# A fused three-layer transformer kernel: reordered splits in the last two differential heads, a reordered delta-rule prologue, and both gate projections ahead of the last transposition

## The chip, the cores and the metric

The program runs on one core of one Trainium2 chip. The metric is the device time of one execution in microseconds (us); smaller is better. Several executions of one program are timed, and their median stands for it.

## The reference

One batch of 256 tokens with 1024 channels goes through two layers of a first block (latent attention, then differential attention, each followed by a feed-forward network with a three-tap convolution) and one hybrid layer (causal attention and a gated delta rule side by side, joined by gates). Everything is float32. Cut to what the change touches:

```python
def diff_mixer(x, w_qkv, lam_p, subln_g, w_o, layer_idx):   # 8 heads, 2 x 64
    sc = jnp.einsum('bqhjd,bkhjd->bhjqk', qb, k) * scale - slopes * dist
    p = jax.nn.softmax(sc, -1)
    a = p[:, :, 0] - lam * p[:, :, 1]
    o = rms_norm(jnp.einsum('bhqk,bkhd->bqhd', a, v), subln_g) * (1.0 - lam_init)
    return o.reshape(b, s, H * 2 * d) @ w_o

def gated_deltanet(q, k, v, g, beta):                       # 8 heads, chunks of 64
    q, k = l2norm(q) * dk ** -0.5, l2norm(k)
    decay = exp(G[i] - G[j]) for j <= i                     # G: running sum of g
    m = strict_lower((k * beta) @ k.T * decay)
    u, w = solve(I + m, [v * beta, k * beta * exp(G)])
    qk = lower(q @ k.T * decay)
    # then chunk after chunk: v_new = u - w @ S; o = q_dec @ S + qk @ v_new; S = ...

def hybrid_layer(x, ...):
    proj = rmsnorm(x) @ w_in         # q, k, v, z of attention and of the delta rule, gates
    y_a = (attention(q_a, k_a, v_a) * silu(z_a)) @ w_branch_a
    y_b = (rmsnorm(gated_deltanet(silu(conv(...)), g, beta)) * silu(z_b)) @ w_branch_b
    merged = sigmoid(gate_a) * y_a + sigmoid(gate_b) * y_b
    return x + rmsnorm(merged @ w_out)
```

## The kernel before, in words

**Precision and weights.** Each float32 product is made of three TensorE matmuls on a "high" part (the value rounded to a shorter format) and a "low" part (the rest): high by high, high by low, low by high. Every weight matrix comes from memory in chunks of 128 x 1024 into one of six slots (`raw0` to `raw5`). ScalarE writes `high` (line 357), then VectorE or GpSimd writes `low = raw - high` (line 368); this pair is called the split of a chunk. A table of phases (`Phase(...)`) says which slots a stage uses, how many chunks each has, and whose low parts GpSimd makes (`gpsimd_low`; for the differential stage slots 1 and 3, for the following feed-forward stage `ffn1` only slot 3, for the delta rule all). `refill(split, p, k, i)` splits the chunk that follows chunk i of slot k, which is the first of the next stage behind the last.

**What orders the work.** Every engine has a program written out by hand, and runs it in order. Semaphores tell it when a producer is done (`wait_ge`). The SyncE queue (SP) issues the weight loads in order too: a load waits for the low part of the chunk before it in its slot (`low_done`), and all later loads wait behind it.

**Places that the change touches.**

- `diff_pe`, `diff_act`, `diff_dve`, `diff_pool` hold the eight differential heads. Heads 0 to 5 run in `head`, heads a = 6 and b = 7 in `last_heads`. For a head: `scores` (line 1240), VectorE's `take_scores` and `maxima`, ScalarE's `exponentials` (1328), VectorE's `weights` (1425 to 1431, whose end is semaphore `p`), `turn_prob` on TensorE (1248), `take_prob` on ScalarE (1334), `result` (1256), then mean square (1399), root on GpSimd (1488), norm (1404), `turn_result` (1227), `result_high` (1323) and `result_low` (1410), and `add_output` into `acc`. Behind head b stands `rows_out_end` (440 to 448) and the boundary: residual, norm and transposition for the next stage.
- `gdn_pe`, `gdn_act`, `gdn_dve`, `gdn_pool` hold the delta rule. A prologue makes the gates and the inputs of the first pair of heads; then `pair_*` runs four times. In the prologue the convolved q and k are transposed (`turn_pe`, 1754), ScalarE squares them, VectorE sums (`squares_dve`, 1827 and 1828), GpSimd takes the root (`root_pool`, 1902), VectorE scales (`norm_dve`, 1849, semaphore `tk`), TensorE transposes back (`back_pe`, 1769), ScalarE copies (`back_act`, 1808), TensorE multiplies keys and queries (`products_pe`, 1782), VectorE masks (`masked_keys_dve`, 1866), TensorE transposes the mask product (`turn_m_pe`, 1790), ScalarE copies it (`mt_act`, 1813) and VectorE makes the first inverse (`init_rows_dve`, `init_dve`, 1885 to 1898). The mask comes from `decay_dve` (1839 to 1843), `decay_act` (1802) and `mask_pool` (1909 to 1914). `pair_pe` begins with `level_x` (1937), which waits for the last step of `init_dve`. Projections `gdn_block(x, e, j, part)` (1686; x: 0 q, 1 k, 2 v, 3 z; e: head of the pair j; part: half of 24 matmuls) fill the time between. `spin` (505) are matmuls whose result is not used.
- `load_pairs` orders the loads of this stage in the SP queue; slots 0, 1, 2 are q, k, v, slots 3 and 4 the z weights of even and odd heads.
- `att_pe`'s last head (7) of the causal attention: `out_project(pe, 0, ...)`, `att_turn_prob` (2469), `out_project(pe, 1, ...)`, `att_result` (2475). ScalarE's `att_take_prob` stands between the last two.

## Time and profile before

| what | value |
| --- | --- |
| median of 3 executions (lowest, highest) | 1084.79 us (1082.2, 1086.27) |
| the profiled execution's own time | 1084.68 us |
| its span, first to last instruction | 1082.9 us |
| mean granted TensorE clock | 0.991 of full speed |
| TensorE matmul busy | 1046.0 us (97%) |
| VectorE, ScalarE, GpSimd busy | 668.1, 561.0, 417.5 us (62, 52, 39%) |
| DMA | 162.27 MB, mean 150 GB/s |
| chain that ended last, by engine | PE 79%, POOL 6%, issue 6%, DVE 5%, ACT 3%, DMA 2% |

The span is the stretch from the first to the last instruction; 1.8 us of the execution lie around it. PE is TensorE, DVE VectorE, ACT ScalarE, POOL GpSimd. TensorE is busy nearly throughout, so what is left to look for are the few stretches in which it idles or runs at a lower granted clock. An overlapped matmul's duration is longer than its distance to the next one.

### The profile page before, as it was taken

What the parts mean: (1) busy time and instruction counts of PE and PEld (TensorE: products, weight loads), DVE (VectorE), ACT (ScalarE), POOL (GpSimd) and SP (SyncE); (2) the same over time, 40 slices, a digit from 0 to 9 for tenths busy, and PEclk for the clock granted to TensorE, in tenths of its full rate; (3) what the DMA queues carried; (4) which work ended last, traced back from release to release, by engine and by line L of the source; (5) the groups of instructions that cost most, each with busy time, mean ns of one, the idle gap of its engine ahead of it and who ended that gap; (6) DMA issues with size and microseconds to landing.
All of it is one profiled execution on the core that took longest, in us unless ns stands there. A gap on an engine that the chain in (4) does not pass through costs nothing.

```text
span 1082.9 us, 21787 instructions
## 1 busy us (share of the span) xinstructions
PE 1046.0 (97%) x8224; PEld 957.7 (88%) x8224; DVE 668.1 (62%) x1073; ACT 561.0 (52%) x1022; POOL 417.5 (39%) x284
## 2 busy tenths in 40 slices
PE   9899999999999999899999999899999999999997
PEld 7799689999978998599999978799999899999996
DVE  4555766766675556777666755566676555544444
ACT  5455565555564666555555556434533355544443
POOL 1000234334342333333343364656654365534331
PEclk9999999999999999999999999899999999999999
DMA  8334466565544443366655542233323235436551
GB/s 326 118 108 134 147 200 193 177 210 185 178 139 141 149 143 110 103 228 177 205 184 170 173 148 90 98 101 116 99 60 115 82 130 156 152 112 218 191 181 48
DMA packets 46136, 162.27 MB, mean 150 GB/s; under 512 B 5248, under 2 KB 5504, under 8 KB 45952
## 3 DMA queue, kind: packets, MB, share of 16 engines
q1 hardware_dynamic: 44784, 156.78, 44.2%
q0 software_dynamic: 1296, 4.72, 1.5%
q8 instruction: 38, 0.62, 0.2%
q14 instruction: 18, 0.15, 0.0%
HBM read 160.43 MB, written 1.05 MB: 149 GB/s over the span
## 4 chain that ended last, share of the span: by engine, by line
PE 79%; POOL 6%; issue 6%; DVE 5%; ACT 3%; DMA 2%; SPq 0%; DVEq 0%; POOLq 0%; ACTq 0%
PE work L399 12%; PE work L401 12%; PE work L400 12%; PE work L1686 8%; PE acc L399 5%; PE acc L400 5%; PE acc L401 5%; PE work L2407 4%; POOL low L368 4%; PE work L2419 2%; PE acc L2419 2%; PE acc L1951 1%; PE acc L1937 1%; ACT high L357 1%; PE acc L1953 1%
## 5 line engine op out<-in xcount | busy, mean ns | idle before, releaser
L368 POOL TENSOR_TENSOR low<-raw,high 128x1024 fp32r<-128x1024 f32 x109 | 264.8, 2432 | 303.5 <-ACT high L357 303.5
L368 DVE TENSOR_TENSOR low<-raw,high 128x1024 fp32r<-128x1024 f32 (+3 forms) x183 | 272.7, 1498 | 163.3 <-ACT high L357 163.2
L357 ACT ACTIVATE high<-raw 128x1024 fp32r<-128x1024 f32 (+2 forms) x293 | 299.8, 1032 | 47.3 <-DMA raw<-in_w_out 26.1
L399 PE MATMUL work<-xh,high 128*128 128x256 f32 (+1 forms) x1032 | 291.6, 283 | 0.7 <-DVE low L368 0.7
L400 PE MATMUL work<-xl,high 128*128 128x256 f32 (+1 forms) x1032 | 288.8, 280 | 0.0
L401 PE MATMUL work<-xh,low 128*128 128x256 f32 (+1 forms) x1032 | 288.7, 280 | 0.0
L399 PEld LDWEIGHTS work<-xh,high 128*128 128x128 f32 (+1 forms) x1032 | 194.2, 188 | 7.7 <-issue 4.8
L400 PEld LDWEIGHTS work<-xl,high 128*128 128x128 f32 (+1 forms) x1032 | 194.3, 188 | 2.3 <-issue 0.6
L401 PEld LDWEIGHTS work<-xh,low 128*128 128x128 f32 (+1 forms) x1032 | 194.1, 188 | 0.2
L1157 POOL TENSOR_TENSOR h<-gelu,cv 128x256 f32<-128x256 f32 x44 | 49.2, 1118 | 202.1 <-ACT gelu L1077 108.3
L1686 PE MATMUL work<-xh,high 128*128 128x256 f32 x256 | 77.4, 302 | 2.2 <-DVE hn L1741 2.2
L1686 PE MATMUL work<-xl,high 128*128 128x256 f32 x256 | 72.5, 283 | 0.0
L1686 PE MATMUL work<-xh,low 128*128 128x256 f32 x256 | 72.3, 282 | 0.0
L399 PE MATMUL acc<-high,hh 128*128 128x512 f32 x168 | 66.0, 393 | 2.0 <-DVE low L368 1.2
L400 PE MATMUL acc<-low,hh 128*128 128x512 f32 x168 | 65.9, 392 | 0.0
L401 PE MATMUL acc<-high,hl 128*128 128x512 f32 x168 | 65.4, 390 | 0.0
L1083 ACT ACTIVATE hh<-h 128x256 fp32r<-128x256 f32 x44 | 18.4, 418 | 70.2 <-POOL h L1157 70.2
L1686 PEld LDWEIGHTS work<-xh,high 128*128 128x128 f32 x256 | 48.8, 191 | 4.9 <-issue 2.4
L1071 ACT ACTIVATE cv<-work,vec 128x256 f32<-128x256 f32 x44 | 24.8, 564 | 51.0 <-PE work L401 51.0
L1686 PEld LDWEIGHTS work<-xh,low 128*128 128x128 f32 x256 | 49.0, 191 | 0.0
L1686 PEld LDWEIGHTS work<-xl,high 128*128 128x128 f32 x256 | 48.9, 191 | 0.0
L1159 POOL TENSOR_TENSOR hl<-h,hh 128x256 fp32r<-128x256 f32 x44 | 34.4, 782 | 24.4 <-ACT hh L1083 24.4
(386 smaller groups left out, 2220.9 us busy)
## 6 DMA issues: line engine op xcount, KB each, us to landing
raw<-in_w_ffn SPq DMA_DIRECT2D x132, 512.0 KB, 4.3
raw<-in_w_out SPq DMA_DIRECT2D x39, 512.0 KB, 4.4
raw<-in_w_att SPq DMA_DIRECT2D x32, 512.0 KB, 3.7
raw<-in_w_diff SPq DMA_DIRECT2D x31, 512.0 KB, 4.2
raw<-in_w_gdn SPq DMA_DIRECT2D x24, 512.0 KB, 3.7
raw<-in_w_mla SPq DMA_DIRECT2D x8, 512.0 KB, 3.5
raw<-in_w_gdnz SPq DMA_DIRECT2D x8, 512.0 KB, 3.6
raw<-in_w_mla SPq DMA_DIRECT2D x8, 384.0 KB, 3.1
```

Of the source, the lines that this page charges most:

```text
L357: act.activation(high[k][:, 0:w], raw[k][:, 0:w], ACT.Copy).then_inc(high_done[k], 1)
L368: eng.tensor_tensor(low[k][:, 0:w], raw[k][:, 0:w], high[k][:, 0:w], ALU.subtract).then_inc(low_done[k], 1)
L399: pe.matmul(out, lhs[0], rhs[0], start=start, stop=False)
L400: pe.matmul(out, lhs[0], rhs[1], start=False, stop=False)
L401: return pe.matmul(out, lhs[1], rhs[0], start=False, stop=stop)
L1071: act.activation((cg, cv)[value][j][:], W[bank][:, 0:TOK], ACT.Identity, scale=ffn_taps(layer, i, j, value, 1, 0), bias=ffn_taps(layer, i, ...
L1083: act.activation(hh[j][:], h32[j][:], ACT.Copy).then_inc(f[j]["hh"], 1)
L1157: pool.tensor_tensor(h32[j][:], gelu[j][:], cv[j][:], ALU.mult).then_inc(s["h32"], 1)
L1159: pool.tensor_tensor(hl[j][:], h32[j][:], hh[j][:], ALU.subtract).then_inc(s["hl"], 1)
L1686: last = pe.matmul(W[x][:, 0:TOK], l[slot][:, b * P:(b + 1) * P], r[:, b, :], start=(s == 0), stop=(s == 23))
L2407: last = pe.matmul(W[0][:, t * TOK:(t + 1) * TOK], x[:, b, t * P:(t + 1) * P], w[k][:, o:o + TOK], start=(b == 0 and term == 0), stop=(b = ...
L2419: last = pe.matmul(out, w[k][:, b * P:(b + 1) * P], x[:, b, :], start=(s == 0), stop=(s == 23))
```

## The change

It edits four places. (1) In the last two differential heads ScalarE takes the transposed probabilities before it splits the first feed-forward chunk of slot 0, and its other splits move one place later; GpSimd no longer makes the low part for the first `ffn1` chunk of slot 1 (VectorE does, behind `result_low(b)`), and it waits for head b's `weights` before the low part of slot 3. (2) In the delta rule's prologue the orders of TensorE, ScalarE, VectorE and GpSimd change, four spin matmuls go, and the copy of the gate rows is cut in two functions. (3) The load of slot 2's third chunk is issued one place earlier. (4) In the last attention head both gate projections stand ahead of the transposition of the probabilities.

```diff
@@ -1359,21 +1359,21 @@
             exponentials(a)
             take_qk(b, W[1])
             result_high(a - 1, W[0][:, TOK:2 * TOK])
+            take_prob(a, W[1])
             refill(split, ph["diff"], 0, b)
-            take_prob(a, W[1])
-            refill(split, ph["diff"], 1, b)
             squares(a)
             exponentials(b)
             refill(split, ph["diff"], 3, a - 1)
-            split(ph["ffn1"], 4, 0)
+            refill(split, ph["diff"], 1, b)
             take_values(b)
             take_prob(b, W[2])
             result_high(a)
             squares(b)
             refill(split, ph["diff"], 2, b)
-            split(ph["ffn1"], 5, 0)
+            split(ph["ffn1"], 4, 0)
             result_high(b)
             refill(split, ph["diff"], 3, a)
+            split(ph["ffn1"], 5, 0)
 
         act.wait_ge(d["lam"], 1)
         refill(split, ph["diff"], 0, 0)
@@ -1471,6 +1471,7 @@
             result_norm(b)
             refill(split, ph["diff"], 2, b)
             result_low(b)
+            refill(split, ph["diff"], 1, b)
 
         dve.wait_ge(d["lam"], 5)
         for k in (0, 1):
@@ -1497,9 +1498,8 @@
                 refill(split, ph["diff"], 3, i - 1)
 
         def last_heads(a, b):
-            pool.wait_ge(high_done[1], ph["ffn1"].base[1] + 1)
-            pool.tensor_tensor(low[1][:], raw[1][:], high[1][:], ALU.subtract).then_inc(low_done[1], 1)
             result_root(a)
+            pool.wait_ge(h["p"], b + 1 + DIFF_SEEN)
             refill(split, ph["diff"], 3, a - 1)
             result_root(b)
 
@@ -1578,7 +1578,10 @@
 
     def gates_rows_act(act):
         act.wait_ge(z_["pe"], 3)
+        act.wait_ge(e_["cums"], 1)
         act.activation(cum_all[:], acc[:].rearrange("p a (c k) -> p (a c) k", c=4), ACT.Copy).then_inc(z_["act"], 1)
+
+    def gates_grown_act(act):
         act.activation(grown_all[:], acc[:].rearrange("p a (h t k) -> p (a h) t k", h=2, t=NT)[:, :, 1, :],
                        ACT.Exp).then_inc(z_["act"], 1)
 
@@ -1840,6 +1843,8 @@
         if not is0(j):
             dve.wait_ge(e_["be"], j)
         dve.tensor_scalar(dec_l[:], dcum, 0.0, None, ALU.max)
+        if is0(j):
+            squares_dve(dve, 0)
         dve.tensor_scalar(dec_u[:], dcum, 0.0, None, ALU.min).then_inc(e_["dd"], 1)
 
     def norm_dve(dve, j):
@@ -1878,8 +1883,6 @@
         masked_dve(dve, 1).then_inc(e_["mk"], 1)
 
     def init_rows_dve(dve, j):
-        if is0(j):
-            dve.memset(inv_t[HALF:P, :, 0:HALF], 0.0)
         dve.wait_ge(e_["mk"], 2 * j + 1)
         for h_ in HALVES:
             last = dve.tensor_tensor(bm[h_, 0, :, 0:HALF].rearrange("p (e t) k -> p e t k", e=2), mk[h_, :, 0, :, h_],
@@ -2074,13 +2077,11 @@
         turn_pe(pe, 0)
         block_pe(pe, 3, 0)
         block_pe(pe, 2, 1)
+        back_pe(pe, 0)
         gdn_block(pe, 3, 1, 0, 0)
-        back_pe(pe, 0)
+        products_pe(pe, 0)
+        turn_m_pe(pe, 0)
         gdn_block(pe, 3, 1, 0, 1)
-        products_pe(pe, 0)
-        spin(pe, A[1], 2)
-        turn_m_pe(pe, 0)
-        spin(pe, A[1], 2)
         for i in range(PAIRS):
             pair_pe(pe, i)
 
@@ -2169,15 +2170,16 @@
         block_high_act(act, split, 1, 1, 0)
         for e in range(2):
             squares_act(act, 0, e)
-        decay_act(act, 0)
         gates_rows_act(act)
         z_tanh_act(act, 0, 0)
-        block_high_act(act, split, 3, 0, 0)
+        decay_act(act, 0)
+        gates_grown_act(act)
         block_mid_act(act, 2, 1, 0)
         back_act(act, 0)
+        block_high_act(act, split, 3, 0, 0)
+        mt_act(act, 0)
         z_tanh_act(act, 1, 0)
         block_high_act(act, split, 2, 1, 0)
-        mt_act(act, 0)
         block_high_act(act, split, 3, 1, 0)
         for i in range(PAIRS):
             pair_act(act, i)
@@ -2298,15 +2300,15 @@
         block_taps_dve(dve, 1, 1, 0)
         block_silu_dve(dve, 1, 1, 0)
         decay_dve(dve, 0)
-        gates_key_dve(dve)
-        squares_dve(dve, 0)
         z_silu_dve(dve, 0, 0)
         norm_dve(dve, 0)
-        z_silu_dve(dve, 1, 0)
+        gates_key_dve(dve)
+        dve.memset(inv_t[HALF:P, :, 0:HALF], 0.0)
         masked_keys_dve(dve, 0)
         init_rows_dve(dve, 0)
         init_dve(dve, 0)
         masked_queries_dve(dve, 0)
+        z_silu_dve(dve, 1, 0)
         for i in range(PAIRS):
             pair_dve(dve, i)
 
@@ -2364,10 +2366,10 @@
         block_low_pool(split, 1, 1, 0)
         root_pool(pool, 0)
         mask_pool(pool, 0)
+        pool.wait_ge(e_["init_g"], 1)
+        grow_pool(pool, 0)
         block_low_pool(split, 3, 0, 0)
         block_low_pool(split, 2, 1, 0)
-        pool.wait_ge(e_["init_g"], 1)
-        grow_pool(pool, 0)
         block_low_pool(split, 3, 1, 0)
         for i in range(PAIRS):
             pair_pool(pool, i)
@@ -2501,10 +2503,9 @@
                     att_queries_keys(pe, i + 1, part)
             else:
                 out_project(pe, 0, 0, xh, xl)
-            att_turn_prob(pe, i)
-            if not more:
                 pe.wait_ge(h["vev"], HEADS + ATT_SEEN)
                 out_project(pe, 1, 0, xh, xl)
+            att_turn_prob(pe, i)
             if more:
                 for part in range(2):
                     att_values(pe, i + 1, part)
@@ -2878,11 +2879,14 @@
                     for k in (0, 1):
                         if c > 2:
                             load(sp, p, k, c)
+                if j == 0:
+                    load(sp, p, 2, 2)
                 if j + 2 < PAIRS:
                     load(sp, pz, 3, j + 2)
                 else:
                     load_first(ph["att"], 3)
-                load(sp, p, 2, 2 * j + 2)
+                if j > 0:
+                    load(sp, p, 2, 2 * j + 2)
                 if j + 2 < PAIRS:
                     load(sp, pz, 4, j + 2)
                 load(sp, p, 2, 2 * j + 3)
```

What the order of instructions becomes is shown at three places. First GpSimd in the last two differential heads, behind the loop (`COMPARE_AND_BRANCH`); line 1488 (1489 after) is the root of a head, 368 a low part. Before:

```order
L466 COMPARE_AND_BRANCH
L1501 TENSOR_TENSOR low<-raw,high 128x1024
L1488 TENSOR_TENSOR stat<-mean,vec 128x2
L368 TENSOR_TENSOR low<-raw,high 128x1024
L1488 TENSOR_TENSOR stat<-mean,vec 128x2
L601 TENSOR_TENSOR stat<-mean,vec 128x1 x2
```

and with the change:

```order
L466 COMPARE_AND_BRANCH
L1489 TENSOR_TENSOR stat<-mean,vec 128x2
L368 TENSOR_TENSOR low<-raw,high 128x1024
L1489 TENSOR_TENSOR stat<-mean,vec 128x2
L601 TENSOR_TENSOR stat<-mean,vec 128x1 x2
```

The first low part is gone from GpSimd, and the root of head a comes first. Second, VectorE in the prologue, from the decay differences to the masked keys. Before:

```order
L1839 TENSOR_TENSOR bm<-acc,gate_cum 128x512
L1842 TENSOR_SCALAR dec_l<-bm 128x512
L1843 TENSOR_SCALAR dec_u<-bm 128x512
L1611 TENSOR_TENSOR gate_bg<-gate_eg,gate_beta 128x16
L1827 TENSOR_REDUCE ssq<-sq 128x8
L1828 TENSOR_SCALAR mean<-ssq 128x8
L1741 SCALAR_TENSOR_TENSOR hn<-tanh_z,work 128x256
L1849 TENSOR_TENSOR qk_tok<-work,root 128x512 x2
L1741 SCALAR_TENSOR_TENSOR hn<-tanh_z,work 128x256
L1866 TENSOR_TENSOR mk<-acc,mask_e 128x2x256
```

and with the change:

```order
L1842 TENSOR_TENSOR bm<-acc,gate_cum 128x512
L1845 TENSOR_SCALAR dec_l<-bm 128x512
L1830 TENSOR_REDUCE ssq<-sq 128x8
L1831 TENSOR_SCALAR mean<-ssq 128x8
L1848 TENSOR_SCALAR dec_u<-bm 128x512
L1744 SCALAR_TENSOR_TENSOR hn<-tanh_z,work 128x256
L1854 TENSOR_TENSOR qk_tok<-work,root 128x512 x2
L1614 TENSOR_TENSOR gate_bg<-gate_eg,gate_beta 128x16
L2306 MEMSET inv_t 64x4x64
L1871 TENSOR_TENSOR mk<-acc,mask_e 128x2x256
```

The sum of squares and its mean now stand between the two decay parts, and the second gate silu (`hn`) leaves the stretch. Third, ScalarE in the same prologue, from the squares to the copy of the transposed mask product. Before:

```order
L1796 ACTIVATE sq<-work 128x512 x2
L1802 ACTIVATE dec_l<-dec_l 128x512
L1803 ACTIVATE dec_u<-dec_u 128x512
L1581 ACTIVATE cum_all<-acc 128x2048
L1582 ACTIVATE grown_all<-acc 128x1024
L1711 ACTIVATE tanh_z<-work 128x256
L357 ACTIVATE high<-raw 128x1024
L1696 ACTIVATE conv<-work,vec 128x256
L1808 ACTIVATE silu<-work 128x2x256
L1809 ACTIVATE silu<-work 128x2x256
L1711 ACTIVATE tanh_z<-work 128x256
L357 ACTIVATE high<-raw 128x1024
```

and with the change:

```order
L1799 ACTIVATE sq<-work 128x512 x2
L1582 ACTIVATE cum_all<-acc 128x2048
L1714 ACTIVATE tanh_z<-work 128x256
L1805 ACTIVATE dec_l<-dec_l 128x512
L1806 ACTIVATE dec_u<-dec_u 128x512
L1585 ACTIVATE grown_all<-acc 128x1024
L1699 ACTIVATE conv<-work,vec 128x256
L1811 ACTIVATE silu<-work 128x2x256
L1812 ACTIVATE silu<-work 128x2x256
L357 ACTIVATE high<-raw 128x1024
L1816 ACTIVATE mt<-work 128x512
L1714 ACTIVATE tanh_z<-work 128x256
```

The large copy `cum_all` moves ahead of the exponentials, and a split that stood ahead of the copy-back (`silu`, lines 1808 and 1811) now stands behind it.

## Rows read from the trace of the kernel before

**Rows 1.** Waits of TensorE, whole run: who waited <- whom: us, times, longest
```profile
PE work L515 <- DVE hn L547: 4.6, 6, 1.9
...
PE acc L1937 <- DVE inv L1898: 1.7, 1, 1.7
```

**Rows 2.** Windows: stretch, length, busy of PE, PEld, DVE, ACT, POOL; granted clock, DMA share, GB/s
```profile
425.00:430.00 5.00, 3.08 (x23) 2.36 (x22) 4.41 (x9) 3.30 (x6) 0.00 (x0) 1.00 0.80 314
438.03:441.57 3.54, 3.36 (x16) 2.99 (x17) 1.37 (x4) 1.07 (x2) 0.00 (x0) 0.55 0.41 143
700.00:704.00 4.00, 3.98 (x46) 3.71 (x48) 2.37 (x5) 0.39 (x1) 3.47 (x3) 0.65 0.02 4
964.00:968.00 4.00, 4.00 (x23) 4.00 (x22) 0.82 (x1) 0.49 (x1) 0.00 (x0) 0.57 0.79 262
700.01:744.12 44.11, 44.10 (x520) 41.55 (x520) 27.94 (x59) 17.59 (x32) 25.58 (x17) 0.96 0.31 97
744.12:787.16 43.04, 43.04 (x527) 40.53 (x526) 30.63 (x63) 19.66 (x35) 27.49 (x18) 1.00 0.32 99
```

**Rows 3.** Timeline of PE, last heads: start, duration, [idle before <- releaser]
```profile
428.85 0.35 PE L1256 MATMUL work<-v_sb,prob_t 128*128 128x128 f32 x1 [1.30 <-issue]
...
438.03 0.44 PE L1248 MATMUL work<-const,prob 128*128 128x128 f32 x2 [2.48 <-DVE prob L1431]
```

**Rows 4.** Lines L1399 and L1428 on DVE: ns min/median/max over all heads
```profile
L1399 DVE TENSOR_SCALAR mean<-stat x8: 169/171/1957, 347.2 to 442.6; 128x2 f32<-128x2 f32 x8
...
L1428 DVE TENSOR_SCALAR prob<-prob,soft x16: 347/353/2453, 340.7 to 434.6; 128x256 f32<-128x256 f32 x16
```

**Rows 5.** Timeline of POOL, last heads
```profile
430.40 2.40 POOL L1501 TENSOR_TENSOR low<-raw,high 128x1024 fp32r<-128x1024 f32 x1 [8.32 <-ACT high L357]
...
434.47 2.44 POOL L368 TENSOR_TENSOR low<-raw,high 128x1024 fp32r<-128x1024 f32 x1
```

**Rows 6.** Timeline of ACT, last heads and the first row of the boundary behind them
```profile
427.21 1.06 ACT L357 ACTIVATE high<-raw 128x1024 fp32r<-128x1024 f32 x1 [1.17 <-DMA raw<-in_w_ffn]
...
428.18 0.58 ACT L1334 ACTIVATE prob_t<-work 128x512 f32<-128x512 f32 x1
...
432.20 0.50 ACT L1328 ACTIVATE prob<-prob,soft 128x256 f32<-128x256 f32 x1
...
447.24 0.60 ACT L574 ACTIVATE xh<-acc 128x512 fp32r<-128x512 f32 x1 [0.86 <-PE acc L448]
```

**Rows 7.** Timelines of the prologue: PE, DVE, POOL, DVE, ACT, ACT
```profile
687.07 0.36 PE L1686 MATMUL work<-xh,high 128*128 128x256 f32 x1 [2.22 <-DVE hn L1741]
...
679.70 2.62 DVE L1843 TENSOR_SCALAR dec_u<-bm 128x512 f32<-128x512 f32 x1
...
683.83 1.68 POOL L1902 TENSOR_TENSOR root<-mean,vec 128x8 f32<-128x8 f32 x1 [1.78 <-DVE mean L1828]
...
686.84 1.28 DVE L1849 TENSOR_TENSOR qk_tok<-work,root 128x512 f32<-128x512 f32 x2
...
691.22 0.60 ACT L1808 ACTIVATE silu<-work 128x512 f32<-128x512 f32 x1 [3.44 <-PE work L1769]
...
696.96 1.06 ACT L357 ACTIVATE high<-raw 128x1024 fp32r<-128x1024 f32 x1 [3.95 <-DMA raw<-in_w_gdn]
```

**Rows 8.** The same steps in the second pair: chain of waits (products), then timeline of DVE
```profile
737.84 1.79 PE acc L1782 x16
...
739.66 0.69 DVE L1866 TENSOR_TENSOR mk<-acc,mask_e 128x512 f32<-128x512 f32 x1 [1.84 <-PE acc L1782]
...
743.03 0.42 DVE L1898 TENSOR_TENSOR inv<-const,work 128x256 f32<-128x256 f32 x1
```

**Rows 9.** DVE instructions with two operands in SBUF: L1858 by line, one L368 by timeline
```profile
L1858 DVE TENSOR_TENSOR kdec<-qk_tok,gate_kd x4: 416/416/418, 705.9 to 834.6; 128x256 f32<-128x256 f32 x4
...
940.32 2.20 DVE L368 TENSOR_TENSOR low<-raw,high 128x1024 fp32r<-128x1024 f32 x1 [1.39 <-ACT high L357]
```

**Rows 10.** Timeline of PE, last attention head
```profile
963.74 0.67 PE L2469 MATMUL work<-const,causal_prob 128*128 128x128 f32 x3 [2.04 <-DVE causal_prob L2641]
```

## The prediction

> **What bounds the kernel.** I read the shares of busy time first: TensorE is busy for 97% of the span, so only its idle stretches and its clock can give time back. The list of its waits comes next. Its largest entry belongs to the boundaries between stages (4.6 us in six waits), which the change does not edit; of the others, the one ahead of the first pair of the delta rule is 1.7 us long [rows 1]. Its timeline shows the rest: 1.30 us and 2.48 us in the last two differential heads [rows 3], 2.22 us in the prologue [rows 7], 2.04 us in the last attention head [rows 10]. Then I read windows for the granted clock. After three of them (2.48, 1.73, 2.04 us) the clock falls from 1.00 to a mean of 0.55 to 0.65, that is to its lower level of 1.2 GHz, for about 4 us; after 1.30 us it stays at 1.00 [rows 2]. So each long idle costs twice: the first pair of heads takes 44.11 us, the next one 43.04 us [rows 2].
>
> **Part 1, the last two differential heads.** TensorE's transposition of head b's probabilities waits 2.48 us, to 438.03 [rows 3]. What makes them late is VectorE: a mean that takes 0.17 us in most heads once took 1.96 us, and a scaling of 0.35 us once took 2.45 us [rows 4]. Both lie against a GpSimd low part: 430.40 to 432.80 and 434.47 to 436.91 [rows 5]. The change takes the first off GpSimd and puts the second behind these weights. VectorE then has 1.8 + 2.1 = 3.9 us less to do. Part of the 1.8 is hidden by ScalarE's exponentials, which end at 432.7 [rows 6]; behind them stand about 2 us of short VectorE work, so the weights are ready near 434.7. TensorE itself is free at 438.03 - 2.48 = 435.55 [rows 3], or, since ScalarE's copy of head a's probabilities no longer stands behind a split (it started at 428.18, after one that began at 427.21 [rows 6], while the transposition ended at 427.55), 0.55 us earlier: 435.0. The wait vanishes. First term: 2.5 + 0.55 = 3.0 us.
>
> The low clock behind it goes as well. The stretch 438.03 to 441.57 ran at 0.55 [rows 2]; it is a chain of short transpositions, copies and one product. At full clock I take 2.4 us for its 3.54: half as long would be 1.8, unchanged 3.5. Second term: 1.1 us (bounds 0 and 1.7).
>
> Price: ScalarE now has two splits behind `result_high(b)`, before one. It was idle 0.86 us there [rows 6], a split takes 1.06 us, and the load for the first of them is issued when GpSimd's low part ends (436.91, which is not earlier than before). I take 0.3 us (bounds 0 and 1). VectorE's added low part stands in the same idle time ahead of `acc`: nothing, and if that cover is gone, at most its 1.2 us. Slot 1's next load waits for it but stands behind slot 2's in the queue: nothing. Part 1: 3.0 + 1.1 - 0.3 = 3.8 us.
>
> **Part 2, the prologue.** Before, the squares' mean stood behind the second decay part, which waited on GpSimd's third low part and ended at 679.70 + 2.62 = 682.32; the root began at 683.83 [rows 7]. Now the sum (some 1.2 us) stands ahead of it, so the mean is out when that low part ends, at 682.2 to 682.6. From there the chain is: root 1.7 (to 684.3), norm 1.28 (685.5) [rows 7], transposition back 0.9 (686.4), ScalarE's two copies 2 x 0.6 [rows 7] less their overlap (687.5), products 1.8 [rows 8] (689.4), and from the masking to the first inverse what the second pair shows, 739.66 to 743.45 = 3.8 [rows 8]. The first `level_x` starts at 693.2 at the latest and 692.9 at the earliest, against 700.01. ScalarE's copy of the gate rows now runs while VectorE sums, and the mask, GpSimd's next work behind the root, has the 5 us until the products end. TensorE has 4.8 us of projections and products in there and idles three times, 0.7, 0.9 and 0.8 us: shorter than the 1.30 after which the clock stayed. The spins (3.8 us of busy time) are no work and cost nothing to leave out. First term: 7.0 us. Second: the first pair at full clock, 44.11 - 43.04 = 1.1 us [rows 2].
>
> Price: GpSimd now does three low parts (7.1 us) without a pause from 692.4, where `kdec` and `kbg` follow at 697.1, just as the third begins. The row of `kdec` shows 0.416 to 0.418 us in all pairs, never beside a low part; a VectorE low part that met one took 2.20 us [rows 9], one alone 1.2. By the first row the price is 0, by the second up to 2.3 us on VectorE, of which TensorE's half projection hides about 1.1. I take 1.1, because `kdec` reads two SBUF tiles as the low part does. The Trainium skill ("SBUF — State Buffer", section "SBUF: two separate sides") says that a VectorE instruction with two SBUF inputs and a GpSimd instruction that reads SBUF lock each other out for a whole instruction. By that rule the price stands; by the `kdec` row alone the sum would be 1.1 us larger.
>
> The load of slot 2's third chunk no longer waits behind slot 3's, for which ScalarE waited 3.95 us, to 696.96 [rows 7], before it could copy the transposed mask product. Its gain is inside the 7.0. Slot 3's load is issued 3 us later, at 694.7, some 20 us before its split. Nothing. Part 2: 7.0 + 1.1 - 1.1 = 7.0 us.
>
> **Part 3, the last attention head.** The second gate projection covers the 2.04 us wait that ended at 963.74 [rows 10]: TensorE reaches the transposition at 964.2. What is late next is ScalarE's copy behind it, an idle of 0.6 us. The 24 matmuls of the second projection took 4.6 us at a mean clock of 0.57 [rows 2], against 3.15 for the first. Sum: 2.04 + 1.45 - 0.6 + 0.3 (the slow transposition) = 3.2 us; bounds 2 and 3.5.
>
> **Sum.** 3.8 + 7.0 + 3.2 = 14.0 us. From the profiled execution's 1084.68 us (0.1 below the median) that gives 1070.7 us. The scatter of the three executions, 4 us, is wider than 0.1, and a change under 0.5% (5.4 us) cannot be told from none.
>
> **Rivals.** (A) The clock falls all the same. The new prologue has three idles within 8 us and the spins are gone. For it: 1.73 us behind spins was enough at 700 [rows 1, 2]. Against: 1.30 us did not do it. Price: the 1.1 us of the first pair, and about 1.4 us in the prologue: 1073.2 us. The skill ("TensorE: Matmul & The Clock Gate", "What's actually happening") holds that the low level is the default and activity lifts it; that speaks for A, and against taking spins out. (B) Part 1 is given back at the boundary: ScalarE's split, VectorE's low part and a new fall of the clock among short idles take 3 us. 1073.7 us. (C) Only one place works, because another engine holds the other two: about 1081 us. (D) Slower. TensorE's first projection of `ffn1` reads slot 1, whose low part is now the last thing VectorE does before the boundary. If its high part came late, VectorE would block with the whole norm behind it. Each us late costs one, and it decides from 14.0 us late on; by 20 us it is 1090.7 us. For it: nothing is behind it to cover. Against: ScalarE's split of it now stands ahead of `take_values(b)`, near 434.6, some nine us before the low part is due.
>
> **Chances.** Forecast 0.74, A 0.11, B 0.08, C 0.04, D 0.03. Faster by over 0.5%: 0.74 + 0.11 + 0.08 = 0.93. Within 0.5%: 0.04. Slower: 0.03. The range: downwards 1.1 (`kdec` free), 0.9 (upper bounds of parts 1 and 3) and 2.2 for a boundary that escapes its low clock by the shift in time, to 1066.5; upwards A and B together (5.5) and 1 us of scatter, to 1077.2.
>
> **What would show it.** Right: no wait of TensorE over 1 us ahead of lines 1248 and 2471 (before 2469); lines 1399 and 1428 without their long cases; the first `level_x` some 7 us closer to the prologue's first transposition (line 1757; 21.8 us before); the first pair within 0.3 us of the second; a mean clock of 1.00 in all three places. Wrong: GpSimd low parts that still end where VectorE's short instructions end; a first pair of 44 us; a wait on a DMA ahead of ScalarE's splits; a boundary behind the differential heads longer than before.

## The result and the profile after

The changed kernel takes **1071.45 us** (median of four runs, 1068.46 to 1072.0), the kernel before 1084.91 us on the same chip (four runs, 1082.2 to 1086.27). The ratio is 0.9875, with a 95% interval of 0.9859 to 0.9892: faster by 13.5 us, 11.7 to 15.3. The forecast was 1070.7. The profiled execution took 1071.75 us with a span of 1069.9, 13.0 less than the span before.

The head of the page, and TensorE's waits over the whole run (columns as in [rows 1]):

```profile
span 1069.9 us, 21773 instructions
```
```profile
PE work L515 <- DVE hn L547: 4.0, 5, 1.9
PE acc L1954 <- DVE xm L1964: 1.9, 1, 1.9
...
PE acc L1940 <- DVE inv L1901: 0.7, 1, 0.7
```

Of the waits over 1 us that the prediction named none is left above 1 us: ahead of the first pair 0.7 us remains of 1.7 [rows 1], ahead of line 1256 also 0.7 of 1.3 [rows 3]. But the second line is new: 1.9 us inside the first pair, ahead of line 1954, in no view of before.

**The last differential heads**, timelines of PE, DVE, POOL and ACT:

```profile
434.74 0.60 PE L1248 MATMUL work<-const,prob 128*128 128x128 f32 x4
...
437.31 0.48 PE L399 MATMUL acc<-high,oh 128*128 128x512 f32 x1
...
430.31 0.16 DVE L1399 TENSOR_SCALAR mean<-stat 128x2 f32<-128x2 f32 x1
430.38 1.22 DVE L368 TENSOR_TENSOR low<-raw,high 128x1024 fp32r<-128x1024 f32 x1
...
433.02 0.61 DVE L1428 TENSOR_SCALAR prob<-prob,soft 128x256 f32<-128x256 f32 x2
433.67 0.88 DVE L1431 SCALAR_TENSOR_TENSOR prob<-prob,soft 128x256 f32<-128x256 f32 x2
...
430.55 1.60 POOL L1489 TENSOR_TENSOR stat<-mean,vec 128x2 f32<-128x2 f32 x1 [8.52 <-DVE mean L1399]
434.63 2.36 POOL L368 TENSOR_TENSOR low<-raw,high 128x1024 fp32r<-128x1024 f32 x1 [2.48 <-DVE prob L1431]
...
440.93 2.00 ACT L357 ACTIVATE high<-raw 128x1024 fp32r<-128x1024 f32 x2
442.83 0.60 ACT L574 ACTIVATE xh<-acc 128x512 fp32r<-128x512 f32 x1
```

GpSimd's low part now starts behind the weights, VectorE's mean takes 0.16 us and its scaling 0.61 for two, and head b's transposition starts at 434.74 without a wait, 3.29 us earlier than in [rows 3]. The boundary's first row comes at 442.83 against 447.24 [rows 6]: 4.41 us earlier. Of these 3.29 lie ahead of head b's transposition, 0.97 between it and the first output product at 437.31 (2.57 us for 3.54 [rows 2]), and 0.15 behind that. ScalarE went from its second split straight into it, so the extra split took nothing.

**The prologue and the first pair**, timelines of DVE, POOL and PE:

```profile
676.61 0.43 DVE L1831 TENSOR_SCALAR mean<-ssq 128x8 f32<-128x8 f32 x1
...
684.64 0.69 DVE L1871 TENSOR_TENSOR mk<-acc,mask_e 128x512 f32<-128x512 f32 x1 [3.92 <-PE acc L1785]
...
692.54 2.27 DVE L1863 TENSOR_TENSOR kdec<-qk_tok,gate_kd 128x256 f32<-128x256 f32 x1
694.73 2.60 DVE L1864 TENSOR_TENSOR kbg<-qk_tok,gate_bg 128x256 f32<-128x256 f32 x1
697.25 0.41 DVE L1964 TENSOR_TENSOR xm<-acc,const 128x256 f32<-128x256 f32 x1
...
677.12 1.79 POOL L1905 TENSOR_TENSOR root<-mean,vec 128x8 f32<-128x8 f32 x1
...
687.45 7.07 POOL L368 TENSOR_TENSOR low<-raw,high 128x1024 fp32r<-128x1024 f32 x3
694.70 2.35 POOL L368 TENSOR_TENSOR low<-raw,high 128x1024 fp32r<-128x1024 f32 x1 [0.17 <-ACT high L357]
...
673.14 1.05 PE L1757 MATMUL work<-const,silu 128*128 128x128 f32 x8
...
680.28 1.09 PE L1772 MATMUL work<-const,qk_tok 128*128 128x128 f32 x8 [0.48 <-DVE qk_tok L1854]
...
688.19 0.68 PE L1940 MATMUL acc<-inv,mt 64*64 64x64 f32 x16 [0.75 <-DVE inv L1901]
...
697.72 0.33 PE L1954 MATMUL acc<-xm,inv 64*64 64x64 f32 x4 [1.90 <-DVE xm L1964]
```

The chain to the first `level_x` is the one forecast. The root starts 3.98 us behind the prologue's first transposition (677.12 - 673.14), against 5.63 before (683.83 [rows 7] - 678.20), and `level_x` 15.05 us behind it, against 21.81. ScalarE waits for no DMA in it. Behind it `kdec` takes 2.27 us and `kbg` 2.60, where [rows 9] has 0.42 for `kdec` in all pairs: one lies against the third of three low parts, the other against a fourth, of slot 0, that GpSimd begins 0.17 us after the third. (By the program the three are the next chunks of slots 3, 2 and 4; the fourth is `block_low_pool(split, 0, 0, 1)`, the first line of `pair_pool`.) `xm` comes behind both, and TensorE waits 1.90 us for it.

Part of the 6.76 us (21.81 - 15.05) is clock. The prediction names falls of the clock behind three idles; there was a fourth, behind the 2.22 us in the prologue. The transposition back ran in it (mean clock 0.57 from 687 to 691); timeline of PE of the kernel before:

```profile
689.35 1.83 PE L1769 MATMUL work<-const,qk_tok 128*128 128x128 f32 x8
```

With the change the same eight matmuls take 1.09 us.

**The last attention head**, timeline of PE, and **windows** (columns as in [rows 2]):

```profile
954.57 0.49 PE L2471 MATMUL work<-const,causal_prob 128*128 128x128 f32 x3
955.63 0.70 PE L2477 MATMUL work<-causal_t,v_sb 128*128 128x256 f32 x2 [0.58 <-ACT causal_t L2559]
...
956.31 0.36 PE L399 MATMUL work<-obh,high 128*128 128x256 f32 x1
```
```profile
434.74:437.31 2.57, 2.14 (x19) 1.70 (x17) 1.25 (x4) 1.46 (x3) 2.26 (x1) 1.00 0.00 0
684.00:688.19 4.19, 2.66 (x22) 2.30 (x21) 3.36 (x8) 1.31 (x3) 1.43 (x2) 1.00 0.01 2
...
696.00:700.00 4.00, 2.28 (x38) 2.22 (x39) 3.93 (x7) 0.39 (x1) 1.05 (x1) 0.88 0.96 373
700.00:704.00 4.00, 4.00 (x36) 3.65 (x34) 1.31 (x4) 1.42 (x2) 0.91 (x1) 0.70 0.03 9
688.19:734.23 46.04, 44.14 (x521) 41.46 (x521) 32.03 (x60) 19.18 (x34) 28.45 (x17) 0.96 0.32 104
734.23:777.27 43.04, 43.04 (x525) 40.52 (x524) 30.58 (x63) 19.66 (x35) 27.47 (x18) 1.00 0.32 99
954.00:958.00 4.00, 3.42 (x28) 3.13 (x27) 1.44 (x2) 1.44 (x4) 0.45 (x1) 1.00 0.75 262
```

The clock is at its full level in the three places where it had fallen to a mean of 0.55 to 0.65. It falls in one new place, behind the new wait, and the first pair takes 46.04 us, more than before, where it was 44.11 [rows 2].

**Where the 13.0 us are.** At the boundary behind the differential heads 4.41 are gained. The prologue's first transposition stands at 673.14 against 678.20, 5.06 earlier: 0.65 more. The first `level_x` stands at 688.19 against 700.01, 11.82 earlier: 6.76 more. The first pair gives 1.93 back, and the later pairs start 43.02 to 43.05 us apart in both kernels. The last projection of the attention moves from 969.06 to 956.31, 12.75 earlier, 2.92 of it within part 3. The end adds 0.2.

The 0.65 us lie in a stretch that the change does not touch. Between `ffn1` and the delta rule TensorE waits 1.9 us in both kernels, but the low clock behind it begins and ends at different instructions. The same 24 matmuls took 3.69 us before and 3.12 after. One window of each kernel, at the same place in the program or close to it, first before, then after:

```profile
656.00:660.00 4.00, 4.00 (x29) 2.69 (x28) 1.21 (x3) 0.19 (x2) 0.00 (x0) 0.89 0.01 4
```
```profile
651.57:655.57 4.00, 4.00 (x34) 3.24 (x33) 1.22 (x3) 0.53 (x2) 0.00 (x0) 1.00 0.00 0
```

This is no steady effect of the change. From the boundary's first row to the prologue's first transposition the profiled executions of all fourteen kernels take 229.6 to 231.1 us; in e4, e5, e9 and e11 of the experiments below (229.6 to 229.7) the clock doesn't fall there at all, behind the same idle of 1.9 us.

### The profile page after: what moved, and what is told of

The parts are those of the page before. It is cut to its first block, busy times and chain, and to the rows that moved or that the text cites. A ratio compares the mean times of both kernels' runs of the same rounds, so it can differ in the third digit from the quotient of the medians.

```text
span 1069.9 us, 21773 instructions
## 1 busy us (share of the span) xinstructions
PE 1038.2 (97%) x8216; PEld 951.9 (89%) x8216; DVE 667.1 (62%) x1074; ACT 561.4 (52%) x1022; POOL 415.5 (39%) x283
## 3 DMA queue, kind: packets, MB, share of 16 engines
q1 hardware_dynamic: 44784, 156.78, 44.6%
## 4 chain that ended last, share of the span: by engine, by line
PE 89%; DVE 4%; POOL 3%; ACT 3%; issue 1%; DVEq 0%; ACTq 0%
PE work L399 13%; PE work L401 13%; PE work L400 13%; PE work L1689 8%; PE acc L399 6%; PE acc L400 6%; PE acc L401 6%; PE work L2409 4%; PE work L2421 2%; PE acc L2421 2%; POOL low L368 1%; PE acc L1954 1%; PE acc L1940 1%; ACT high L357 1%; PE acc L1956 1%
## 5 line engine op out<-in xcount | busy, mean ns | idle before, releaser
L368 POOL TENSOR_TENSOR low<-raw,high 128x1024 fp32r<-128x1024 f32 x109 | 264.8, 2433 | 297.7 <-ACT high L357 295.2
L368 DVE TENSOR_TENSOR low<-raw,high 128x1024 fp32r<-128x1024 f32 (+2 forms) x184 | 274.0, 1497 | 163.5 <-ACT high L357 163.4
```

The costliest lines, as they stand in the source:

```text
L368: eng.tensor_tensor(low[k][:, 0:w], raw[k][:, 0:w], high[k][:, 0:w], ALU.subtract).then_inc(low_done[k], 1)
```

## The experiments

Each ratio is to the kernel before, run on the same chip, with its 95% interval. Where a difference is given by the ratios and by the medians, the two differ by the scatter of the runs.

**One part at a time.** The first three kernels are the kernel before with one part of the change each: the hunks on the last differential heads; those on the prologue, with the load; the two lines in the last attention head.

e1 has the hunks at 1359, 1471 and 1497, with this wait among them:

```diff
+            pool.wait_ge(h["p"], b + 1 + DIFF_SEEN)
```

e2 has all hunks from 1578 to 2364 and the one at 2878, with these lines among them:

```diff
+        if is0(j):
+            squares_dve(dve, 0)
```

e3 has the hunk at 2501:

```diff
-            att_turn_prob(pe, i)
-            if not more:
                 pe.wait_ge(h["vev"], HEADS + ATT_SEEN)
                 out_project(pe, 1, 0, xh, xl)
+            att_turn_prob(pe, i)
```

> The kernel before with part 1 alone (the last two differential heads). Theory (sum of independent terms): against the kernel before it saves what the trace of the changed kernel shows up to the boundary behind the heads, 4.4 us (447.24 to 442.83 for the first row of the boundary), so about 1080.5 us. Rival (the boundaries' low clock depends on when they are reached): another 0 to 1.5 us either way, 1079 to 1082 us. The low clock at 438 is gone in the trace.

> The kernel before with part 2 alone (prologue of the delta rule and the one load). Theory: 6.8 us up to the first level_x, less 2.0 us in the first pair, where kdec and kbg wait for GpSimd: 4.8 us saved, 1080.1 us. Rival (the long first pair comes from part 1's shift in time or from the granted clock's own rhythm, not from the two waits): the first pair takes 43.0 to 44.1 us here and 6.8 to 7.8 us are saved, 1077 to 1078 us.

> The kernel before with part 3 alone (both gate projections ahead of the last transposition). Theory: 3.0 us saved, 1081.9 us, idle ahead of att_result near 0.6 us and a granted clock of 1.00 from 960 to 968. Rival (the wait only moves to ScalarE's copy or to the split of slot 1): under 1.5 us saved, over 1083.4 us.

Measured, against 1084.2 us before: e1 1080.88, ratio 0.9956 (0.9942 to 0.9969), 4.8 us by the ratio and 3.3 by the medians; e2 1077.12, 0.9933 (0.992 to 0.9947), 7.3 and 7.1 us; e3 1081.92, 0.9977 (0.9968 to 0.9986), 2.5 and 2.3 us. All three parts work alone. Together they make 14.6 us by the ratios and 12.7 by the medians, where the whole change makes 13.5.

e1 and e3 came out as their theories said. e2 did not: it saved some 7 us where the theory had 4.8, and though the rival's time came, its first pair did not (44.57 us, outside 43.0 to 44.1). In e2 the keys meet GpSimd as in the changed kernel, and TensorE waits as long, but the clock stays. Timeline of DVE, then a window of e2 (TensorE's wait ended at 703.06):

```profile
697.88 2.28 DVE L1863 TENSOR_TENSOR kdec<-qk_tok,gate_kd 128x256 f32<-128x256 f32 x1
700.08 2.59 DVE L1864 TENSOR_TENSOR kbg<-qk_tok,gate_bg 128x256 f32<-128x256 f32 x1
```
```profile
704.00:708.00 4.00, 4.00 (x50) 3.60 (x46) 2.81 (x7) 1.81 (x3) 0.65 (x1) 1.00 0.33 132
```

Its first pair takes 44.57 us, from 693.54 to 738.11. So the wait costs 1.9 us each time, and the low clock behind it 1.5 us (46.04 - 44.57) in one kernel and nothing in another.

The clock also stays in the last attention head of e2, which has the old order and the old wait there. Timeline of PE and a window of e2, to be held against [rows 10] and the mean clock of 0.57 in [rows 2]:

```profile
957.83 0.55 PE L2471 MATMUL work<-const,causal_prob 128*128 128x128 f32 x3 [2.03 <-DVE causal_prob L2643]
```
```profile
958.00:962.00 4.00, 4.00 (x34) 3.95 (x34) 1.03 (x2) 0.49 (x1) 0.00 (x0) 1.00 0.71 262
```

From this transposition to the last projection e2 takes 3.77 us (957.83 to 961.60), the kernel before 5.32 (963.74 to 969.06). So in the profiled execution 1.5 us of what e2 saves is clock in the place of part 3, and the three parts can't simply be added.

**The keys ahead of the collision.** e4 is the changed kernel with `kdec` and `kbg` of the first pair in the prologue, where VectorE waits 3.92 us for the products. e11 does the same for all pairs. The edit of e4:

```diff
         dve.memset(inv_t[HALF:P, :, 0:HALF], 0.0)
+        scaled_keys_dve(dve, 0)
         masked_keys_dve(dve, 0)
...
-        scaled_keys_dve(dve, i)
+        if i > 0:
+            scaled_keys_dve(dve, i)
```

e11 drops the last two lines, and has behind `z_silu_dve(dve, 1, i + 1)` of each pair:

```diff
+            scaled_keys_dve(dve, i + 1)
             masked_keys_dve(dve, i + 1)
```

> The changed kernel, with the first pair's kdec and kbg moved into the prologue, where VectorE waits 3.9 us for the products. Theory (the two waits for GpSimd's low parts cost 1.9 us of TensorE idle and a stretch at the low clock behind it): the first pair takes 43.0 us instead of 46.0, and the time is 3.0 us lower than the changed kernel's, 1068.4 us. Rival (VectorE has enough slack, and the pair is long for the clock's sake alone): under 1 us lower. Second rival (kdec delays GpSimd's mask and with it the products' masking): higher than the changed kernel by up to 1 us.

> As with kdec and kbg in the prologue, and in all four pairs they stand ahead of the masking instead of in the level chain. Theory (the pair's levels are paced by VectorE's chain, as the first pair's 42.6 us against 43.04 us of the others shows): all four pairs take 42.6 us: 1.3 us below the kernel with the first pair's keys early, 1067.5 us. Rival (TensorE paces the pairs): the later pairs stay at 43.04 us, 1068.5 to 1069 us.

e4 took 1069.15 us against 1084.2, ratio 0.9854 (0.9839 to 0.987), e11 1067.74 against 1085.64, 0.9844 (0.9816 to 0.9872). In the prologue the two keys of e4 take 1.10 and 0.83 us beside GpSimd's mask, inside VectorE's idle time, and the first `level_x` comes as far behind the first transposition as in the changed kernel (15.03 us): the second rival of e4 did not happen. The new wait is gone from both kernels, and the first pair takes 42.63 us in e4 (688.60 to 731.23) and 42.61 in e11: 3.4 us less than in the changed kernel, the 1.9 of the wait and the 1.5 of the clock. e11's later pairs take 43.05 and 43.04 us, as with the keys in their old place: there the keys met no low part, and taking them out of VectorE's chain of levels changes nothing. So its theory was wrong and the rival right, though the time of 1067.74 us is the theory's (1067.5). The profiled execution of e11 shows where such a time can come from without it: the clock did not fall between `ffn1` and the delta rule.

**Which of the two collisions costs.** e8 takes only `kdec` ahead. e9 leaves both keys where they are and makes GpSimd's third low part wait until `xm` is out. e8, in the prologue (`scaled_keys_dve` leaves the same line out for pair 0):

```diff
+        dve.wait_ge(z_["act"], 6)
+        dve.wait_ge(e_["tk"], 1)
+        dve.tensor_tensor(kdec[:], qk_tok[:, :, 2, :], spread(gate_at("kd", 0, chunk=0), P), ALU.mult)
         masked_keys_dve(dve, 0)
```

e9:

```diff
         block_low_pool(split, 2, 1, 0)
+        pool.wait_ge(e_["xm"], 2)
         block_low_pool(split, 3, 1, 0)
```

> The changed kernel, with kdec alone moved into the prologue; kbg stays. Theory (the first collision is hidden by TensorE's half projection, only the second costs): kbg waits from 692.5 to the end of the third low part at 694.5, the mask product of the next level comes 2.2 us late where 1 to 2.5 us are covered: the first pair takes 42.6 to 43.2 us, 1069.1 to 1069.8 us, as with both moved. Rival (each collision costs the same): half of the gain, 1070.3 us, first pair 44.3 us.

> The changed kernel, with GpSimd's third low part behind the prologue waiting for the second level's mask product, so that kdec and kbg meet no low part. Theory (the long kdec and kbg are GpSimd's low parts and nothing else): both take 0.42 us at their old place, the wait of 1.9 us goes, the first pair takes 43.0 us, 1068.8 us. Rival (they are long for another reason, the port being taken by DMA or ScalarE): they stay over 2 us.

e8 took 1068.31 us against 1083.71, 0.9856 (0.9832 to 0.988). e9 took 1068.29 against 1085.64, 0.9847 (0.9819 to 0.9875). Timeline of DVE of e8:

```profile
692.51 2.27 DVE L1865 TENSOR_TENSOR kbg<-qk_tok,gate_bg 128x256 f32<-128x256 f32 x1
694.70 0.41 DVE L1965 TENSOR_TENSOR xm<-acc,const 128x256 f32<-128x256 f32 x1
```

One key still lies against the low part for 2.27 us, yet TensorE does not wait and the first pair takes 42.56 us. So one collision is covered, and the whole loss comes with the second. In e9 neither happens, and GpSimd's pause of 2.13 us costs nothing (first pair 42.65 us). Both theories held, and the times are 0.5 to 0.8 us below theirs. Timelines of DVE and POOL of e9:

```profile
692.36 0.42 DVE L1863 TENSOR_TENSOR kdec<-qk_tok,gate_kd 128x256 f32<-128x256 f32 x1
...
694.14 4.71 POOL L368 TENSOR_TENSOR low<-raw,high 128x1024 fp32r<-128x1024 f32 x2 [2.13 <-DVE xm L1964]
```

**The load in its old place.** e5 is the changed kernel with slot 2's load behind slot 3's again.

```diff
-                if j == 0:
-                    load(sp, p, 2, 2)
...
-                if j > 0:
-                    load(sp, p, 2, 2 * j + 2)
+                load(sp, p, 2, 2 * j + 2)
```

> The changed kernel, with the load of slot 2's third chunk back behind slot 3's. Theory (the queue holds it until GpSimd's low part of slot 3, which now ends near 689.9): it is issued near 690.2 and lands 4 us later; ScalarE, in order, waits there from 687.8 to 694 with the tanh of the first pair behind it, TensorE idles 3 to 5 us in the first pair and the clock falls: 3 to 6 us above the changed kernel, 1074.5 to 1077.5 us. Rival (nothing in the pair needs ScalarE so soon): within 0.5 us of the changed kernel.

1076.24 us against 1083.71, 0.9929 (0.9905 to 0.9954): slower than the changed kernel by 4.8 us by the medians, 5.9 by the ratios. TensorE's waits, then the timeline of ACT, of e5:

```profile
PE acc L1954 <- DVE xm L1964: 3.2, 1, 3.2
PE work L1764 <- DVE silu L1738: 2.6, 1, 2.6
```
```profile
695.15 2.00 ACT L357 ACTIVATE high<-raw 128x1024 fp32r<-128x1024 f32 x2 [7.39 <-DMA raw<-in_w_gdn]
```

The first `level_x` starts at 688.09 as in the changed kernel, since the copy of the transposed mask product no longer stands behind this split. The price comes one stage later: the first pair takes 50.29 us. That is 4.25 us more than in the changed kernel, nearly all that part 2 brings, and as the theory had it.

**GpSimd's wait for the weights.** e6 takes out `pool.wait_ge(h["p"], ...)`, so that the low part of slot 3 starts as soon as its high part is there. The wait does nothing but hold it back.

```diff
-            pool.wait_ge(h["p"], b + 1 + DIFF_SEEN)
```

> The changed kernel, without GpSimd's wait for head b's weights. Theory (a low part on GpSimd blocks VectorE's scaling and the sum behind it, which reads two SBUF tiles): GpSimd's low part starts near 433.4 and ends near 435.8, the weights end at 436.7 instead of 434.5, TensorE idles 1.5 to 2 us: 1.5 to 3.5 us above the changed kernel, 1073 to 1075 us. Rival (taking the first low part off GpSimd was all that mattered): within 0.5 us.

1073.19 us, 0.9901 (0.9878 to 0.9924): slower than the changed kernel by 1.7 us by the medians, 2.8 by the ratios, with intervals that overlap. Timelines of POOL and DVE of e6:

```profile
433.49 2.38 POOL L368 TENSOR_TENSOR low<-raw,high 128x1024 fp32r<-128x1024 f32 x1 [1.39 <-ACT high L357]
...
433.62 2.92 DVE L1431 SCALAR_TENSOR_TENSOR prob<-prob,soft 128x256 f32<-128x256 f32 x2
```

The low part moves into the weights and the two instructions of line 1431 take 2.92 us for 0.88; TensorE waits 1.7 us ahead of line 1248 again, as the theory said, and no low clock follows there. The boundary comes 1.66 us later and the first `level_x` 2.4 us, but here the clock does not fall in the first pair (44.52 us), which gives 1.5 us of it back.

**ScalarE's copy of the probabilities.** e7 puts one split back ahead of `take_prob(a)`.

```diff
-            take_prob(a, W[1])
             refill(split, ph["diff"], 0, b)
+            take_prob(a, W[1])
```

> The changed kernel, with ScalarE's split of slot 0 again ahead of its copy of head a's transposed probabilities. Theory: the copy starts 0.6 us later and TensorE's two heads with it: 0.6 us above the changed kernel, 1072 us, and a wait of 1.3 us ahead of result(a). Rival (VectorE's chain of head b sets the time, not TensorE): no difference.

1071.97 us, 0.9885 (0.9862 to 0.9908): not to be told from the changed kernel. The wait ahead of line 1256 grows from 0.7 to 1.2 us (1.3 expected), so the 0.5 us is seen in the trace alone.

**The squares' mean behind the second decay part.** e10 undoes the one move on which part 2's chain was said to rest.

```diff
-        if is0(j):
-            squares_dve(dve, 0)
...
         decay_dve(dve, 0)
+        squares_dve(dve, 0)
```

> The changed kernel, with the sum of squares and its mean again behind both decay parts. Theory (the mean's time sets the chain to the first level_x): the root starts near 678.5 instead of 677.1, the transposition back and all behind it 1.4 us later: 1.4 us above the changed kernel, 1072.8 us, and up to 1.5 us more if the clock falls in the longer idle. Rival (another step, the mask, sets the chain): no difference.

1073.94 us against 1085.64, 0.9894 (0.987 to 0.9918): slower than the changed kernel by 2.5 us by the medians, 2.1 by the ratios, though the intervals overlap. Timelines of DVE, POOL and PE of e10:

```profile
674.40 2.65 DVE L1846 TENSOR_SCALAR dec_u<-bm 128x512 f32<-128x512 f32 x1
...
678.46 1.68 POOL L1903 TENSOR_TENSOR root<-mean,vec 128x8 f32<-128x8 f32 x1 [1.69 <-DVE mean L1831]
...
681.51 1.97 PE L1772 MATMUL work<-const,qk_tok 128*128 128x128 f32 x8 [1.95 <-DVE qk_tok L1852]
```

The decay part is caught by the low part again. GpSimd's root starts 5.57 us behind the prologue's first transposition (which stands at 672.89), for 3.98 in the changed kernel. TensorE waits 1.95 us instead of 0.48, and the clock falls behind it: the transposition takes 1.97 us instead of 1.09. The first `level_x` stands 18.08 us behind the first transposition, for 15.05: 3.0 us more, close to the theory's 1.4 and 1.5.

**The spins.** e12 puts both spins back, one behind the products and one ahead of the first pair.

```diff
         products_pe(pe, 0)
+        spin(pe, A[1], 2)
         turn_m_pe(pe, 0)
         gdn_block(pe, 3, 1, 0, 1)
+        spin(pe, A[1], 2)
```

> The changed kernel, with two spin matmuls behind the products and two ahead of the first pair. Theory (the idles of 0.8 us do not make the clock fall, and four spins of 0.9 us a pair are longer than the idles they fill): 1 to 1.5 us above the changed kernel, 1072.5 to 1073 us. Rival A of the prediction (without spins the clock falls more often): at or below the changed kernel's 1071.4 us.

1070.29 us against 1085.64, 0.9863 (0.9835 to 0.9891). The first `level_x` came at 690.34, 2.15 us later (0.53 of it is older than the prologue), as the theory had it, but the total did not follow. Timelines of DVE and POOL of e12:

```profile
694.67 0.65 DVE L1863 TENSOR_TENSOR kdec<-qk_tok,gate_kd 128x256 f32<-128x256 f32 x1
695.25 0.41 DVE L1864 TENSOR_TENSOR kbg<-qk_tok,gate_bg 128x256 f32<-128x256 f32 x1
...
687.99 7.06 POOL L368 TENSOR_TENSOR low<-raw,high 128x1024 fp32r<-128x1024 f32 x3
696.83 2.36 POOL L368 TENSOR_TENSOR low<-raw,high 128x1024 fp32r<-128x1024 f32 x1 [1.79 <-ACT high L357]
```

The keys start 2 us later, when the third low part is nearly over (694.67 against 695.05; `kdec` takes 0.65 us) and the fourth has not begun, and the first pair takes 42.60 us. The spins cost the prologue 1.6 us and save the pair 3.4. The theory missed this, and the time came where the rival had it for another reason than the rival's: it is no effect of the spins on the clock, which was at 1.00 in the prologue without them too.

**The fastest version** is the changed kernel with the keys out of the collision, in any of four forms: e4, e8, e9 and e11 have ratios of 0.9844 to 0.9856, against 0.9875 of the changed kernel. Their profiled spans are 1065.9 to 1067.0 against 1069.9; in three of them (not e8) 0.6 to 0.7 us of that is the clock that did not fall ahead of the delta rule. The four are not to be told apart, and their intervals overlap that of the changed kernel, so the 2 to 3 us rest on the traces (3.4 us in the first pair) more than on the times.

## Why the prediction was right

**Part 1** was to bring 3.8 us and brought 4.4. First term, 3.0: the wait of 2.48 us is gone and the transposition starts 3.29 us earlier. Second, 1.1: the stretch from it to the first output product took 2.57 us for 3.54, at a clock of 1.00, so 0.97. The price of 0.3 was not paid: ScalarE's last split ended as the boundary's first product did. e6 shows that most of the gain hangs on GpSimd's wait for the weights (1.7 us of the wait come back without it), and e1 that the part stands alone; taking the first low part off GpSimd was not tried by itself. Rival B, part 1 given back at the boundary, did not happen: the boundary took 11.58 us from its first row to `ffn1`'s first product in both kernels. The next one, ahead of the delta rule, gave 0.65 us more, by a clock that came back earlier. That term was in no sum, only in the range's lower end, and it is luck.

**Part 2** was to bring 7.0 us and brought 4.8. The first term, 7.0 to the first `level_x`, measured 6.76; e10 shows that the mean ahead of the decay part carries 3.0 us of it, and e5 that the load's move is needed, though the gain of the load does not lie where the working put it ("inside the 7.0"): it lies in the first pair, 4 us of it. **The step that failed is the price of 1.1** for `kdec` and `kbg`, as a size. The collision was foreseen, with the right mechanism and the right length for one instruction (2.2 us forecast, 2.27 measured). What was missing is that the second key is caught too, by a fourth low part: the prediction had GpSimd's three low parts and stopped there, though slot 0's split, ScalarE's next one, was done at 694.62 and feeds a fourth that follows at once. Nor was the cover of 1.1 us right: e8 hides a whole collision, and of the 4.0 us that the two keys lost in the changed kernel 2.1 did not reach TensorE. One collision would have cost nothing; two cost 1.9 us, and 1.5 more by the clock behind it (e4 against the changed kernel; e2 and e6 have the wait without the fall). A pair that meets neither takes 42.6 us, so at the 44.1 us that the two terms of 1.1 left it, 1.5 us of collision were allowed for; 3.4 came. The second term, the first pair at full clock, did not come in the changed kernel for that reason. Two of the prediction's own signs went against it here: the first pair was to lie within 0.3 us of the second and lay 3.0 above it, and a first pair of 44 us was named as a sign of being wrong.

The rule weighed against the trace there, from the Trainium skill ("SBUF — State Buffer", section "SBUF: two separate sides"), is borne out: the keys read two SBUF tiles and waited for whole low parts. Its words, that whichever of the two starts first gets the shared pair of ports "for the whole instruction", also fit the second loss: the fourth low part started at 694.70, the second key at 694.73.

**Rival A**, the clock falls all the same, was wrong in the prologue (three idles of 0.48, 0.78 and 0.75 us, clock 1.00) and came true in the first pair, but by a new wait and not by the missing spins. e12, whose prologue ran at the same clock with the spins, shows no difference by them; behind an idle of 1.95 us without spins, in e10, it did fall.

**Part 3** was to bring 3.2 us and brought 2.92, with ScalarE's copy late by 0.58 us where 0.6 was taken; e3 gives 2.5 us, 1.5 to 3.5. Its clock term, 1.45 us and 0.3 for the slow transposition, holds against an execution in which the clock falls there; in e2 it stayed up behind the same wait, and only the wait itself would have been left to gain.

**Rivals C and D** fell: each part alone gives its gain, and slot 1's low part, the last before the boundary on VectorE, ended at 442.69, 0.15 us before the boundary's first instruction could start there, and TensorE's first projection of `ffn1` did not wait for it.

The terms' errors, +0.6, +0.65, -2.2 and -0.3 with 0.2 at the end, cancel in part: 13.0 for 14.0 of span. The right total is in part luck. In the range, the upper bounds of parts 1 and 3 as the working gives them add up to 1.2 us and not 0.9 (0.6 and 0.3 in part 1, 0.3 in part 3), which would put the lower end at 1066.2.

## What to carry to other kernels

A move that lets a queue of low parts run without a pause is to be followed past the instructions it was made for: list what each engine starts next, and look for the short VectorE instructions that then fall on GpSimd's work; the cure is to move these few into an idle stretch, or to hold one GpSimd instruction back. Of several collisions in a row only the one that uses up the cover costs. A total that comes out right says little about its terms: check each against its row. And a part measured by itself can hold a clock gain that belongs to another place: look at the granted clock over the whole run before adding parts.

## What the runs showed of the hardware

- The lock between VectorE and GpSimd holds two ways. GpSimd's root took 1.60 us beside a VectorE low part (430.55 against 430.38), and 0.70 where it stood alone (438.50, head b).
- A short VectorE instruction can lose twice in a row: 0.42 us became 2.27 and then 2.60, a low part having started 0.03 us ahead of the second.
- The two instructions of line 1431, with two SBUF inputs, took 2.92 us for 0.88 when a low part began 0.13 us ahead of them (e6).
- Which VectorE instructions are caught differs. `dec_u`, with one SBUF input, took 2.65 us beside a low part (e10) and 0.42 without (the changed kernel, 676.95). The sum over `sq` took 1.22 us beside a low part (the changed kernel, 675.35) and 1.21 without (e10, 676.97): that is why it could move ahead. `xm`, with one of its inputs in PSUM, took 0.41 us at 694.70 in e8 beside a low part that began at 694.66.
- The same idle of 1.90 us at the same instruction brought the low clock in the changed kernel, e7 and e10 (first pair 46.0 to 46.1 us), and not in e2 and e6 (44.6 and 44.5 us). An idle of 2.04 us ahead of the last attention head's transposition brought it in the kernel before, one of 2.03 us in e2 did not. The idle's length alone does not decide it; what does, no run here shows.
